# Attention with stationary values: two heads in the array's column halves, output born transposed, long and short query blocks in turn

## The reference

```python
def causal_attention(q, k, v):            # q,k (B,S,H,96); v (B,S,H,64)
    scale = QK_HEAD_DIM ** -0.5
    def block(i):                         # 128 queries
        sc = jnp.einsum('bhqd,bhkd->bhqk', qb, k).astype(jnp.float32) * scale
        sc = jnp.where(kpos[None, :] <= qpos[:, None], sc, -jnp.inf)
        p = jax.nn.softmax(sc, axis=-1).astype(v.dtype)
        return jnp.einsum('bhqk,bhkd->bhqd', p, v)
```

## Time and profile before

| | us |
|---|---|
| median of 3 runs | 1969.71 (1968.88 to 1987.22) |
| the profiled execution, its own time | 1968.05 |
| its span | 1966.1 |
| attention stage: first matmul to end of the last copy | 867.57 to 1055.31 |

### The profile page before, as it was taken

The page is one execution under the profiler, slowest core; times in us unless marked ns, Lnnn a source line. Parts: engine busy times, 40 slices in busy tenths (PEclk is TensorE's granted clock), DMA queues, the critical chain, the costliest instruction groups (busy, mean ns, idle before and its releaser), DMA issues. The chain is left out here.

```text
span 1966.1 us, 31165 instructions
## 1 busy us (share of the span) xinstructions
PE 1603.4 (82%) x12790; PEld 1165.7 (59%) x12790; DVE 815.4 (41%) x1212; ACT 490.2 (25%) x829; POOL 275.5 (14%) x294
## 2 busy tenths in 40 slices
PE   5799978778878645779996999999950899999990
PEld 2688843677767422458885888787840454454440
DVE  0623358565566626656565101355153112112124
ACT  0611131222223233333334222221040122222220
POOL 0000010454355001310000000000003111111103
PEclk9899988899999877769998999999975899999995
DMA  7511141000000547000003111312041899999958
GB/s 260 176 44 43 44 178 43 3 3 3 3 3 3 178 162 291 1 0 1 1 1 150 54 43 53 129 43 96 1 197 58 350 384 361 367 361 370 364 224 342
DMA packets 69541, 264.71 MB, mean 135 GB/s; under 512 B 7205, under 2 KB 15925, under 8 KB 55350
## 3 DMA queue, kind: packets, MB, share of 16 engines
q1 hardware_dynamic: 55850, 219.57, 29.6%
q0 software_dynamic: 8832, 26.27, 3.4%
q10 hardware_dynamic: 4752, 17.30, 2.2%
HBM read 208.42 MB, written 54.71 MB: 134 GB/s over the span
## 5 line engine op out<-in xcount | busy, mean ns | idle before, releaser
L2100 PE MATMUL ps<-gu,xT 128*128 128x512 f32 x528 | 237.9, 597 | 0.9 <-ACT xT L2148 0.9
L2100 PEld LDWEIGHTS ps<-gu,xT 128*128 128x128 f32 x528 | 98.5, 192 | 112.7 <-issue 112.7
L343 PE MATMUL ps<-hs,wh 128*128 128x512 f32 x320 | 126.8, 396 | 17.0 <-DVE hs L339 13.3
L2192 DVE TENSOR_TENSOR sg<-sg,ps 128x256 f32<-128x256 f32 x33 | 13.9, 420 | 292.4 <-ACT sg L2153 292.4
L345 PE MATMUL ps<-hs,wl 128*128 128x512 f32 x320 | 126.3, 395 | 0.0
L2112 PE MATMUL ps<-dn,hidT 128*128 128x512 f32 x264 | 118.7, 592 | 0.0
L344 PE MATMUL ps<-hs,wh 128*128 128x512 f32 x256 | 100.3, 392 | 0.0
L339 DVE TENSOR_TENSOR wl<-wraw,wh 128x1024 fp32r<-128x1024 f32 x24 | 29.4, 1225 | 154.7 <-ACT wh L336 154.7
L343 PE MATMUL ps<-hh,wr_h 128*128 128x512 f32 x224 | 88.6, 396 | 0.0
L344 PE MATMUL ps<-hl,wr_h 128*128 128x512 f32 x224 | 88.6, 396 | 0.0
L345 PE MATMUL ps<-hh,wr_l 128*128 128x512 f32 x224 | 88.6, 395 | 0.0
(11 more groups left out here) (340 smaller groups left out, 3391.1 us busy)
## 6 DMA issues: line engine op xcount, KB each, us to landing
gu<-w_e_gate SPq DMA_DIRECT2D x33, 1024.0 KB, 8.5
gu<-w_e_up SPq DMA_DIRECT2D x33, 1024.0 KB, 11.7
dn<-w_e_down SPq DMA_DIRECT2D x33, 1024.0 KB, 6.2
expert_rows<-YTM ACTq DMA_DIRECT2D x33, 512.0 KB, 8.9
wada<-w_ada SPq DMA_DIRECT2D x8, 2048.0 KB, 11.9
expert_rows<-zrow SPq DMA_DIRECT2D x4, 4096.0 KB, 31.3
wbuf<-w_ada SPq DMA_DIRECT2D x4, 2048.0 KB, 16.6
wraw<-w_gates SPq DMA_DIRECT2D x16, 512.0 KB, 3.5
```

The lines of the kernel that those rows point to most:

```text
L343: nc.tensor.matmul(out, wt[0], mov[0], start=(k == 0), stop=False)
L2100: last = nc.tensor.matmul(ps[:, GB[b]], xT[:, b, k], gu[:, b, :, k], start=(k == 0), stop=(k == KD - 1))
```

## The change

- The scale moves from the exponentials to the queries' gain (GpSimd, before this stage), and the peak is negated by the reduction itself, so the small VectorE instruction behind each peak is gone.
- The items are ordered by pairs of heads: for q from 0 to 3, for each of the two heads, block 7 - q ("wide") and block q. An item with an even number is wide. Two items of the same block in the two heads form a pair; there are 32.
- Wide items' scores use banks 0 and 1, 2 and 3; the others all use bank 6. `prob` has three buffers, `pT` four.
- The mask product's operands are float32r copies, made by two ScalarE instructions at the stage's start; TensorE's first scores wait for them.
- Values: per pair, the values of one head (64 columns) are stationary and the transposed probabilities (128 columns) move; the first head's output goes to partitions 0 to 63 and the second's to 64 to 127 of bank 7. The output is born transposed. The two heads' products take turns block by block.
- Reciprocals per pair (VectorE, 2 columns). GpSimd spreads them over 64 columns each (`rbc`); a product with `rbc` stationary and the identity moving brings them, turned, into the other columns of bank 7. VectorE copies the 256 columns to `ob`, GpSimd multiplies both halves into `YTM`.
- The closing transposes and `orow` are gone. The engines' orders are new.

```diff
@@ -1208,9 +1208,9 @@
             nc.gpsimd.memset(zrow[:], 0.0).then_inc(z_in, 1)
             pool.wait_ge(m_in, 80)
             for i in range(2):
-                nc.gpsimd.tensor_copy(gain[:, i * HEADS:(i + 1) * HEADS],
-                                      g_row[:, i].unsqueeze(1).broadcast_to([P, HEADS, QKD]))\
-                  .then_inc(gain_s, 1)
+                nc.gpsimd.tensor_scalar(gain[:, i * HEADS:(i + 1) * HEADS],
+                                        g_row[:, i].unsqueeze(1).broadcast_to([P, HEADS, QKD]),
+                                        1.0 if i else QKD ** -0.5, None, ALU.mult).then_inc(gain_s, 1)
             pool.wait_ge(gain_s, 2)
             def rope_keys(t):
@@ -1427,27 +1427,58 @@
 with phase() as st:
...
+    prob = sb(st, "prob", [P, 3, SEQ])
+    pT = sb(st, "pT", [P, 4, NT, P])
+    ob = sb(st, "ob", [P, 2, 2 * P])
+    rbc = sb(st, "rbc", [P, 2, 2, N])
+    identr = sb(st, "identr", [P, P], f32r)
+    causalr = sb(st, "causalr", [P, P], f32r)
     nmax = sb(st, "nmax", [P, HEADS * NT])
     rsum = sb(st, "rsum", [P, HEADS * NT])
...
+    masks, s_mm, nm, e_s, rec, rb, tp, tp_d, tp_a, av, o_ev, o_mul = sems(
+        st, "masks", "s_mm", "nm", "e_s", "rec", "rb", "tp", "tp_d", "tp_a", "av", "o_ev", "o_mul")
+    items = [(2 * p + hp, i) for p in range(HEADS // 2) for q in range(NT // 2) for hp in range(2)
+             for i in (NT - 1 - q, q)]
+    pairs = [(p, i) for p in range(HEADS // 2) for q in range(NT // 2) for i in (NT - 1 - q, q)]
+    NI = len(items)
+    def wide(n):
+        return n % 2 == 0
     def wides(n):
...
+        return (n + 1) // 2
+    def pair_of(n):
+        return 2 * (n // 4) + n % 2
+    def items_of(m):
+        n = 4 * (m // 2) + m % 2
+        return n, n + 2
+    def score_bank(n):
+        return (0, 6, 2, 6)[n % 4]
+    def score(n):
+        h, i = items[n]
+        bank = score_bank(n)
+        if wide(n):
+            return ps[:, bank:bank + 2].rearrange("p a n -> p (a n)")[:, 0:(i + 1) * P]
+        return ps[:, bank, 0:(i + 1) * P]
+    def row_sum(n):
+        return 2 * pair_of(n) + (n % 4) // 2
+    OB = 7
     with nc.Block() as block:
         @block.tensor
         def _(pe):
             def scores(n):
                 h, i = items[n]
...
+                back = 4 if wide(n) else 2
+                if n >= back:
+                    pe.wait_ge(e_s, n - back + 1)
+                bank = score_bank(n)
                 q = qkT[0:QKD, h, i * P:(i + 1) * P]
                 kT_ = qkT[0:QKD, HEADS + h]
                 for a in range(0, i * P, 512):
@@ -1456,102 +1487,132 @@
                 at = (i % 4) * P
                 o = ps[:, bank + i // 4, at:at + P]
                 nc.tensor.matmul(o, q, kT_[:, i * P:(i + 1) * P], start=True, stop=False)
...
+                nc.tensor.matmul(o, identr[:], causalr[:], start=False, stop=True).then_inc(s_mm, 1)
             def turn(n):
                 h, i = items[n]
                 pe.wait_ge(e_s, n + 1)
                 if n:
                     pe.wait_ge(tp_d, n)
...
+                if wide(n) and n:
                     pe.wait_ge(tp_a, wides(n))
                 for k in range(i + 1):
                     m = nc.tensor.transpose(ps[:, 4 + k // 4, (k % 4) * P:(k % 4 + 1) * P],
...
+                                            prob[:, n % 3, k * P:(k + 1) * P], C("ident"))
                 m.then_inc(tp, 1)
...
+            def values(m):
+                p, i = pairs[m]
+                two = items_of(m)
+                pe.wait_ge(rb, m + 1)
+                if m:
+                    pe.wait_ge(o_ev, m)
+                nc.tensor.matmul(ps[:, OB, P:2 * P], rbc[:, m % 2].rearrange("p a n -> p (a n)"), C("ident"),
+                                 start=True, stop=True)
+                pe.wait_ge(tp_d, two[1] + 1)
+                if m % 2 == 0:
+                    pe.wait_ge(tp_a, wides(two[1] + 1))
                 for k in range(i + 1):
...
+                    for hp in range(2):
+                        j = nc.tensor.matmul(ps[64 * hp:64 * hp + 64, OB, 0:P], vv[:, k, 2 * p + hp],
+                                             pT[:, two[hp] % 4, k], start=(k == 0), stop=(k == i))
+                j.then_inc(av, 1)
+            pe.wait_ge(masks, 2)
             scores(0)
...
+            scores(1)
+            for n in range(NI):
+                if wide(n) and n + 2 < NI:
+                    scores(n + 2)
                 turn(n)
...
+                if not wide(n) and n + 2 < NI:
+                    scores(n + 2)
+                if n % 4 == 3:
+                    values(n // 4 * 2)
+                if n % 4 == 0 and n:
+                    values(n // 4 * 2 - 1)
+            values(len(pairs) - 1)
+        @block.gpsimd
+        def _(pool):
+            def scaled(m):
+                p, i = pairs[m]
+                pool.wait_ge(o_ev, m + 1)
+                nc.gpsimd.tensor_tensor(YTM[:, p, i * P:(i + 1) * P], ob[:, m % 2, 0:P], ob[:, m % 2, P:],
+                                        ALU.mult).then_inc(o_mul, 1)
+            for m in range(len(pairs)):
+                pool.wait_ge(rec, m + 1)
+                if m >= 2:
+                    pool.wait_ge(av, m - 1)
+                nc.gpsimd.tensor_copy(rbc[:, m % 2],
+                                      rsum[:, 2 * m:2 * m + 2].unsqueeze(2).broadcast_to([P, 2, N]))\
+                  .then_inc(rb, 1)
+                if m >= 2:
+                    scaled(m - 2)
+            scaled(len(pairs) - 2)
+            scaled(len(pairs) - 1)
         @block.scalar
         def _(act):
+            def exponentials(n):
+                h, i = items[n]
+                act.wait_ge(nm, n + 1)
+                if n >= 3:
+                    act.wait_ge(tp, n - 2)
+                at = row_sum(n)
+                nc.scalar.activation(prob[:, n % 3, 0:(i + 1) * P], score(n), ACT.Exp, bias=nmax[:, n:n + 1],
+                                     accum_out=rsum[:, at:at + 1]).then_inc(e_s, 1)
+            nc.scalar.activation(identr[:], C("ident"), ACT.Copy).then_inc(masks, 1)
+            nc.scalar.activation(causalr[:], C("causal"), ACT.Copy).then_inc(masks, 1)
+            exponentials(0)
+            exponentials(1)
             for n, (h, i) in enumerate(items):
...
+                if wide(n):
                     act.wait_ge(tp, n + 1)
...
+                    if n >= 4:
+                        act.wait_ge(av, pair_of(n - 4) + 1)
+                    nc.scalar.activation(pT[:, n % 4, 4:i + 1].rearrange("p k n -> p (k n)"),
                                          ps[:, 5, 0:(i - 3) * P], ACT.Copy).then_inc(tp_a, 1)
+                if n + 2 < NI:
+                    exponentials(n + 2)
         @block.vector
         def _(dve):
             def peak(n):
+                dve.wait_ge(s_mm, n + 1)
+                nc.vector.tensor_reduce(nmax[:, n:n + 1], score(n), AX.X, ALU.max, negate=True).then_inc(nm, 1)
+            def turned(n):
                 h, i = items[n]
...
+                dve.wait_ge(tp, n + 1)
+                if n >= 4:
+                    dve.wait_ge(av, pair_of(n - 4) + 1)
+                k = min(4, i + 1)
+                nc.vector.tensor_copy(pT[:, n % 4, 0:k].rearrange("p k n -> p (k n)"), ps[:, 4, 0:k * P])\
+                  .then_inc(tp_d, 1)
+            def reciprocals(m):
+                dve.wait_ge(e_s, items_of(m)[1] + 1)
+                nc.vector.reciprocal(rsum[:, 2 * m:2 * m + 2], rsum[:, 2 * m:2 * m + 2]).then_inc(rec, 1)
+            def out_rows(m):
+                dve.wait_ge(av, m + 1)
+                if m >= 2:
+                    dve.wait_ge(o_mul, m - 1)
+                nc.vector.tensor_copy(ob[:, m % 2], ps[:, OB, 0:2 * P]).then_inc(o_ev, 1)
             peak(0)
...
+            peak(1)
+            for n in range(NI):
+                if wide(n) and n + 2 < NI:
+                    peak(n + 2)
+                turned(n)
+                if n % 4 >= 2:
+                    reciprocals(pair_of(n))
+                if not wide(n) and n + 2 < NI:
+                    peak(n + 2)
+                if n >= 4 and n % 4 < 2:
+                    out_rows(n // 4 * 2 - 2 + n % 4)
+            out_rows(len(pairs) - 2)
+            out_rows(len(pairs) - 1)
```

More of the change, by code:

```diff
@@ L1433, in build @@
                 nmax = sb(st, "nmax", [P, HEADS * NT])
                 rsum = sb(st, "rsum", [P, HEADS * NT])
-                s_mm, mx, nm, e_s, rec, tp, tp_d, tp_a, av, o_ev, tf, tf_ev = sems(
-                    st, "s_mm", "mx", "nm", "e_s", "rec", "tp", "tp_d", "tp_a", "av", "o_ev", "tf", "tf_ev")
-                items = [(h, i) for h in range(HEADS) for i in range(NT)]
-                wide = [n for n, (h, i) in enumerate(items) if i >= 4]
-                SCALE = QKD ** -0.5
-                def wides(n):
-                    return sum(w < n for w in wide)
+                masks, s_mm, nm, e_s, rec, rb, tp, tp_d, tp_a, av, o_ev, o_mul = sems(
```

(69 more changed lines are left out.)

26 lines of the change are left out of this document (removed).

## The result

The kernel after takes 2003.89 us (median of 4 runs, 2000.1 to 2006.19), the kernel before beside it 1969.39. The forecast was 1978.5, +8.8 us, with a range from 1962 to 2000; the median lies 4 us above that range, and "slower by over 1%" had a quarter of the forecast's chance.

What follows compares the result with a forecast made beforehand. TensorE bounds the attention stage, its work falling but two waits on VectorE added: sixteen rounds of mean 11.94 us give 191.0, the stage ending 8.8 us later; 1968.05 + 8.8 = 1976.9, plus 1.7 gives 1978.5, range 1962 to 2000.

Steps and rivals of the forecast that it cites:

- wait A: Attention: the short pair's values on TensorE wait for VectorE's eviction of the wide pair before, 1.5 us at q = 0.
- wait B: Attention: the second short item's transposes wait for bank 4, until VectorE copies the second wide item, 1.2 us at q = 0.
- Rival 1: Attention: the waits don't bind and TensorE's work does, 42 us less than the forecast, 1936; chance 0.04.
- Emptying: Attention, TensorE: switching between full-width and half-width products costs 0.25 us a pair, 0.5 a round; bounds nothing and 0.55 a pair.
- The restart: Attention: TensorE starts 0.05 us after the VectorE signal it waits for.
- The mask: Attention: a float32r mask product of 128 columns takes 0.11 us, 0.44 a round instead of 0.88.
- The start and the end: Attention: start at 872.5 with the clock rising at 873.4; end at 1064.1, 8.8 us later than before.
- The gain's scaling: GpSimd, before attention: it replaces a copy of the same size long before its first use, costing nothing.
- Rival 2: Attention values: the two column halves run one after the other, 32 us more, 2010; chance 0.10.
- Rival 3: Attention: float32r of 128 columns costs like float32 and the array empties fully, +7.0 + 9.6 us, 1995; chance 0.09.
- Rival 4: Attention: the clock falls in the waits; with half the stage at half clock 234 us instead of 191, 2021; chance 0.06.
- whatever this stage gains or loses moves the rest: Stages after attention: the next stage loads its operands only after attention, so attention's 8.8 us shifts everything behind it.

Runs made afterwards that it cites:

- wait A is gone: Against the kernel after, VectorE evicts the wide pair's output ahead of the next wide item's peak: 1978.78 us, ratio 1.0028.
- without wait B: Against the kernel after, the second wide item's turn precedes the next wide item's scores, and its copy precedes the peak: 1985.62 us, ratio 1.0064.
- without both waits: Against the kernel after, both reorderings together, early eviction of the wide pair and early turn of the second wide item: 1949.11 us, ratio 0.99.

## Why the prediction was right and wrong

**What bounds the stage, and the gain that goes to the waits: right.** Both waits, their places and what queues before them on VectorE (peak W2 and copy W0; the peak of the next W0) came as worked out, and taking each away confirmed it. Their sizes came close: 21.6 / 16 = 1.35 us a round for wait A and 17.8 / 16 = 1.1 for wait B, against 1.5 and 1.1 to 1.2, and TensorE idles 2.5 us of a round against 2.6. Rival 1, that they don't bind, did not come. One sign was missed: VectorE's work in a round, forecast as hardly changed, fell from 7.0 to 6.0 us.

**The round: 12.23 us instead of 11.94.** Three terms were off. *Emptying* around the values was taken as 0.25 a pair. For a short pair it is 0.32: the rows of one round give 940.93 - 940.54 = 0.39 for two records of 0.11 and the change to half width (0.17), and 941.30 - 940.93 = 0.37 for 0.22 and the change back (0.15). For a wide pair the same rows give 0.14 and 0.15. That is 0.61 a round, 0.11 more. Not all of it belongs to the width: the step to half width takes 0.10 at the short pairs once wait A is gone, and 0.10 at the wide pairs once the mask product ahead of them is float32. The bound of a whole matmul, 0.55 a pair, was not reached; where the Trainium skill (TensorEngine Tiling, Key Properties) has the engine drain at a change of the tiling mode, this trace shows a cost of 0.14 to 0.17 us each way, and the two edited kernels 0.10 for the first. *The restart* of TensorE on a VectorE signal was taken as 0.05: the eviction ends at 940.39 and the product starts at 940.54; the copy ends at 945.26, the turn starts at 945.40. That is 0.15 and 0.14, on the path twice a round, 0.19 more. The trace of before has both values: 0.055 from VectorE's end to the closing transposes (line 1497, four times), 0.145 to the products of line 933 (eight times). I took the one for the other; what decides between them no run shows. *The mask* was 0.11 and is 0.09, 0.08 less a round. Together that is +0.22 of the 0.29. The 0.29 makes 4.6 us in 16 rounds. *Values and scores* were exact.

**The start and the end: nearly right.** The clock rose at 879.0, not at 873.4. By windows of the kernel after it is 0.50 just before, with TensorE busy throughout, and full just behind:

```profile
871.00:878.80 7.80, 7.80 (x20) 4.72 (x19) 1.72 (x3) 2.11 (x5) 0.00 (x0) 0.50 0.00 0
879.20:890.00 10.80, 8.95 (x78) 7.12 (x76) 4.91 (x11) 4.30 (x10) 0.58 (x2) 1.00 0.01 2
```

Beyond the stage's later start (870.3 against the forecast's 868.1) this is 3.4 us more at half clock, worth some 1.7. With the 4.6 of the rounds that is 6.3, and the stage came out 5.0 over the forecast's 196.0, so the rest of it was 1.3 shorter. I had carried the moment of the rise over from the earlier trace rows as if it stood still. The thirteen traces show what it goes with: it comes 5.8 us after the first scores in the three traces with the old attention and in the kernel without the mask copies, and 8.7 us after them in the nine with the copies, to within 0.03 us, although the stage's start itself scatters by 5.4. So the small step of the copies at the stage's start seems to have moved the rise by 2.9 us: the router's story on a small scale, inside the stage that I had worked out. (The kernel without the copies also has another mask product; the copies were not varied alone.)

**The gain's scaling "a copy of the same size, nothing": wrong in size, right in effect.** The two instructions of the kernel after:

```profile
732.19 4.35 POOL L1211 TENSOR_SCALAR gain<-g_row 128x768 f32<-128x768 f32 x2 [9.96 <-DMA g_lat<-g_kv_a]
```

That is 2.2 us each, where the copy took 0.8 (1.59 for both). They are done long before their first use, so nothing moved.

**Rival 2 (halves in series): did not come, and is now measured**, at 19.5 us where it had 32. The Trainium skill (TensorE: Matmul & The Clock Gate, Part 3) has weight loads overlap with running products only where the row groups differ. Here both halves share all 128 rows and a block of each takes 0.22 together, the time of one, so the measurement decides against the rule for alternating halves; for halves apart it comes near it. **Rival 3**: its first half is measured at 9.0 instead of 7.0 and did not come; its second, full emptying, did not either. **Rival 4** did not come in the kernel after: the granted clock is 1.00 at 81% busy, from 879.0 to the stage's end. It was not empty, though: in two edited kernels (without wait B, and with the float32 mask) the clock fell once for 3.4 us, some 22 us into the stage, at a cost of 1.6 to 1.7 us.

**The step that failed** is a sentence of the first part: "whatever this stage gains or loses moves the rest". The sum took everything behind the attention as shifted, at unchanged length. It was shifted, and for the router that was enough: 16.8 us, more than the attention's own loss. (The kernel before with one fill, whose attention is unchanged, shows the same 40.7.) I had weighed the clock inside the stage that changes, where idle time was added, and nowhere else. The trace of before had the warning in two places: the router's 3.7 us at half clock before the rise, and one of its times at 1987.22, 18 us above the others. By the attention alone the kernel would lie 13 us over before, as it does with the router at full clock (1984.29 against 1971.09), and so within 1%, the likeliest case as forecast; measured it is 34.5, and attention and router are 30.1 of the 36.5 between the profiled executions. That a quarter of the chance stood on "slower" is no credit: the rivals behind it, 2 to 4, did not come, and the router was in none of them.

**Open.** What sets off the rise in the router at one start and withholds it at a start a microsecond later is not settled: runs show that a shift turns it, not by what rule. One number goes with it. In the two traces whose router is fast without added products (the kernel before, and the one without both waits) the clock behind the gates fell 2.1 us after their last product; in the nine with a slow router it fell 3.7 to 4.7 us after it, and the fill moved it from 2.1 to 4.5. The kernel after with thirteen products has 4.5 as well, and its router is fast: so there the added products, and not a lucky place, seem to have held the clock. It is a correlation over thirteen traces; nobody varied it by itself. Nor is it shown why all eight runs of the kernel after fell on the same side while the kernel before had one in five there.

## What to carry to other kernels

When a stage is made shorter at its bounding engine, walk the queues of the engines that free its buffers: here a gain of 24 us became a loss of 13 because an eviction stood one place too late and a transpose one place too late, and moving them gave it back. Half the columns for each of two heads cost nothing extra here when the two heads' products alternate, and 19.5 us when they stand one head behind the other. And a change that merely shifts later stages can move a stage behind it between two clock levels, so read the run times of before for two groups, and look for any stage that starts at half clock after an idle stretch.

## What the runs showed of the hardware that I had not expected

- TensorE without a gap for 36 us (36.00 of 36.00) at a granted clock of 0.50: float32 products of 36 columns and transposes, busy by the profile all the time, did not bring the clock to its upper level. The same work was at full clock from 3.7 us after its start in the kernel before.
- One fill of 1.38 us in one place cost 19 us, in a stage some 390 us later (1971.09 to 1990.38).
- The clock's rise in the attention comes 8.7 us after the first scores in nine traces and 5.8 us after them in four, each to within 0.03 us.
- Eleven products of 512 columns raised the clock, and it fell again after two idle stretches of 1.35 and 1.30 us with eight transposes between them; where the second stretch was filled by a product it held, over 1.90 us of idle time ahead of the first transposes.
- Two products in different column halves, all 128 rows shared, run at once when issued in turn (a weight load every 0.05 us), and nearly in series when not (every 0.09).
- From VectorE's end to the start of a waiting product it is 0.055 us in some places and 0.145 in others, and nothing between (13 traces).
- A float32r product of 128 columns costs 0.09 us where float32 takes 0.22. The change from full to half width costs 0.10 to 0.17 us, the change back 0.14 to 0.15.
